# Four packed products in place of eight in the blockwise triangular inverse of a gated DeltaNet and MoBA block

## What is computed

```python
lower = jnp.where(tri_strict, jnp.einsum('bhnid,bhnjd->bhnij', kbc, kc) * decay, 0.0)
eye = jnp.eye(c, dtype=jnp.float32)
t_mat = lax.linalg.triangular_solve(eye + lower, jnp.broadcast_to(eye, lower.shape),
                                    left_side=True, lower=True, unit_diagonal=True)
u = jnp.einsum('bhnij,bhnje->bhnie', t_mat, vbc)
w = jnp.einsum('bhnij,bhnjd->bhnid', t_mat, kbc * jnp.exp(gc)[..., None])
```

## Time and profile before

| | |
|---|---|
| median of 3 runs | 378.04 us |
| the profiled execution | 377.91 us |
| its span (first to last instruction) | 376.1 us |
| TensorE busy | 365.6 us, 97% |
| VectorE busy | 262.9 us, 70% |
| ScalarE busy | 220.1 us, 59% |
| GpSimd busy | 58.0 us, 15% |

### The profile page before, as it was taken

The page is one execution under the profiler, slowest core; times in us unless marked ns, Lnnn a source line. Parts: engine busy times, 40 slices in busy tenths (PEclk is TensorE's granted clock), DMA queues, the critical chain, the costliest instruction groups (busy, mean ns, idle before and its releaser), DMA issues.

```text
span 376.1 us, 7709 instructions
## 1 busy us (share of the span) xinstructions
PE 365.6 (97%) x2821; PEld 349.4 (93%) x2821; DVE 262.9 (70%) x502; ACT 220.1 (59%) x500; POOL 58.0 (15%) x105
## 2 busy tenths in 40 slices
PE   7999999999999999999999999999999999999993
PEld 5889978899999999999999999999999999999882
DVE  2968977299876767867678577786775557677644
ACT  5776894355456565756657577656676644424531
POOL 3435764510120001002020101001010100000000
PEclk9999999999999999999999999999999999999999
DMA  8849746975986465444655445564446656775532
GB/s 265 227 124 298 263 128 163 243 195 143 235 203 180 119 176 155 112 115 115 173 131 142 114 114 126 136 187 114 113 112 165 174 158 176 195 223 197 218 117 112
DMA packets 99342, 62.57 MB, mean 166 GB/s; under 512 B 3652, under 2 KB 94062, under 8 KB 99310
## 3 DMA queue, kind: packets, MB, share of 16 engines
q1 hardware_dynamic: 98014, 58.72, 56.5%
q0 software_dynamic: 1296, 3.43, 3.1%
HBM read 60.55 MB, written 1.59 MB: 165 GB/s over the span
## 4 chain that ended last, share of the span: by engine, by line
PE 89%; ACT 4%; DVE 3%; issue 1%; DMA 1%; POOL 1%; DVEq 0%; POOLq 0%; ACTq 0%
PE banks L1235 64%; PE banks L1452 6%; PE banks L1252 5%; ACT th_E L666 1%; PE banks L1334 1%; PE banks L1367 1%; PE banks L1372 1%; PE banks L1341 1%; PE banks L1352 1%; DVE acc L925 1%; DMA xin<-in_x_dram 1%; PE banks L1377 1%; ACT h_hi L639 1%; PE banks L1382 1%; DVE w_lo L853 1%
## 5 line engine op out<-in xcount | busy, mean ns | idle before, releaser
L1235 PE MATMUL banks<-h_hi,w_hi 128*128 128x256 f32 x576 | 165.6, 288 | 0.6 <-PE banks L1252 0.3
L1235 PE MATMUL banks<-h_lo,w_hi 128*128 128x256 f32 x576 | 165.5, 287 | 0.0
L1235 PE MATMUL banks<-h_hi,w_lo 128*128 128x256 f32 x576 | 165.1, 287 | 0.0
L853 DVE TENSOR_TENSOR w_lo<-raw,w_hi 128x1024 fp32r<-128x1024 f32 x102 | 124.2, 1221 | 35.2 <-ACT w_hi L626 32.3
L626 ACT CAST w_hi<-raw 128x1024 fp32r<-128x1024 f32 x104 | 107.6, 1045 | 9.6 <-DMA raw<-in_w_in_dram 5.0
L1235 PEld LDWEIGHTS banks<-h_hi,w_hi 128*128 128x128 f32 x576 | 110.0, 191 | 2.1 <-issue 1.8
L1235 PEld LDWEIGHTS banks<-h_hi,w_lo 128*128 128x128 f32 x576 | 110.0, 191 | 0.1
L1235 PEld LDWEIGHTS banks<-h_lo,w_hi 128*128 128x128 f32 x576 | 110.0, 191 | 0.2
L925 DVE SCALAR_TENSOR_TENSOR acc<-banks,vec,acc 128x255 f32<-128x255 f32 (+2 forms) x72 | 34.5, 479 | 10.4 <-ACT acc L722 8.1
L1235 PE MATMUL banks<-y_hi,w_hi 128*128 128x256 f32 x128 | 36.2, 283 | 0.0
L1235 PE MATMUL banks<-y_lo,w_hi 128*128 128x256 f32 x128 | 36.2, 283 | 0.0
(11 more groups left out here) (232 smaller groups left out, 547.2 us busy)
## 6 DMA issues: line engine op xcount, KB each, us to landing
raw<-in_w_in_dram SPq DMA_DIRECT2D x80, 512.0 KB, 5.2
raw<-in_w_branch_dram SPq DMA_DIRECT2D x16, 512.0 KB, 4.4
raw<-in_w_out_dram SPq DMA_DIRECT2D x8, 512.0 KB, 4.2
xin<-in_x_dram SPq DMA_DIRECT2D x2, 512.0 KB, 3.7
xin<-bias_rows POOLq DMA_DIRECT2D x1, 1024.0 KB, 7.5
th_E<-g_rows POOLq DMA_DIRECT2D x2, 512.0 KB, 5.8
raw<-in_x_dram SPq DMA_DIRECT2D x2, 512.0 KB, 3.5
out_dram<-xin SPq DMA_DIRECT2D x4, 256.0 KB, 2.1
```

The lines of the kernel that those rows point to most:

```text
L853: v.tensor_tensor(w_lo[:, t % SLOTS, cols], raw[:, t % SLOTS, cols], w_hi[:, t % SLOTS, cols].bitcast(F32), ALU.subtract).then_inc(s_lo, 1)
L1235: last = mm(ps, w, r, start=i == 0, stop=i == 23)
```

## The change

Each of the four product steps of `stage_u` becomes one product of 128 packed columns on either side. The left operand of the steps s = 1 and s = 6 is a packed copy `lac` of the blocks of `la` that count, which GpSimd makes with two copies of 128 x 128 a head (`compact`); the right operand picks its columns by a strided view. In the result the blocks that are wanted lie scattered over lanes and columns, and VectorE copies them, between lanes where needed, to where they belong. The masks and their multiplications go, and with them two of the tiles of `consts`. `U`'s blocks are written, not added to (they are zero until then).

```diff
+        lac = sb("lac", [P, 2, 2, P])
...
+            def compact(g):
+                if g >= 2:
+                    pool.wait_ge(s_x_p, 2 * g - 2)
+                la = la_all[:, g]
+                pool.tensor_copy(lac[:, g % 2, 0, :].rearrange("p (b c x) -> p b c x", b=2, c=NC),
+                                 la.rearrange("p c (b x) -> p b c x", b=2)[:, :, :, BLK:HALF]).then_inc(s_lac, 1)
+                pool.tensor_copy(lac[:, g % 2, 1, :].rearrange("p (c x) -> p c x", c=NC), la[:, :, HALF:]).then_inc(s_lac, 1)
+                pool.wait_ge(s_lac, 2 * g + 2)
+
+            compact(0)
+            compact(1)
             q_norm(0)
             for g in range(HEADS):
                 o_norm(g)
                 if g + 1 < HEADS:
                     q_norm(g + 1)
+                if g + 2 < HEADS:
+                    compact(g + 2)
...
   VectorE, stage_u
                 s == 2
-                    v.tensor_tensor(xl, chunks(bD[:, 0:256]), copies(C_ML, NC), ALU.mult).then_inc(s_x, 1)
+                    by_block = xl[:, 0, :].rearrange("p (b c j) -> p b c j", b=2, c=NC)
+                    for b in range(2):
+                        v.tensor_copy(by_block[HALF * b + BLK:HALF * b + HALF, :, 0, :],
+                                      bD[HALF * b:HALF * b + BLK, 0:HALF].rearrange("p (b j) -> p b j", b=2)).then_inc(s_x, 1)
+                    v.tensor_copy(by_block[:, :, 1, :], bD[:, HALF:P].rearrange("p (b j) -> p b j", b=2)).then_inc(s_x, 1)
                 s == 5
-                    v.tensor_tensor(U, U, chunks(bD[:, 256:512]), ALU.add).then_inc(s_u, 1)
-                    ve.wait_ge(s_u, 2 * g + 1)
+                    for b in range(2):
+                        for c in range(NC):
+                            lane, col = HALF * b + BLK * c, P + HALF * c + BLK * b
+                            v.tensor_copy(U[HALF * b:HALF * b + BLK, c, HALF * b + BLK:HALF * b + HALF],
+                                          bD[lane:lane + BLK, col:col + BLK]).then_inc(s_u, 1)
+                    ve.wait_ge(s_u, 6 * g + 2)
                 s == 7
-                    v.tensor_tensor(xl[:, :, 0:HALF], bD[:, 0:P].rearrange("p (c n) -> p c n", c=NC),
-                                    copies(C_ML + P, NC)[:, :, 0:HALF], ALU.mult).then_inc(s_x, 1)
+                    for c in range(NC):
+                        v.tensor_copy(xl[HALF:, 1, HALF * c:HALF * c + HALF],
+                                      bD[HALF * c:HALF * c + HALF, 2 * P + HALF * c:2 * P + HALF * c + HALF]).then_inc(s_x, 1)
                 s == 10
-                    v.tensor_tensor(high, high, bD[0:HALF, 256:384].rearrange("p (c n) -> p c n", c=NC),
-                                    ALU.add).then_inc(s_u, 1)
+                    for c in range(NC):
+                        v.tensor_copy(U[0:HALF, c, HALF:],
+                                      bD[HALF * c:HALF * c + HALF, 3 * P + HALF * c:3 * P + HALF * c + HALF]).then_inc(s_u, 1)
...
   TensorE, stage_u
-                    for c in range(NC):
-                        last = mm(bD[:, P * c:P * c + P], la[:, c, :], T[:, c, :], start=True, stop=True)
+                    pe.wait_ge(s_lac, 2 * g + 2)
+                    mm(bD[:, 0:P], lac[:, g % 2, 0, :],
+                       T.rearrange("p c (b x) -> p c b x", b=2)[:, :, :, 0:BLK], start=True, stop=True).then_inc(s_x_p, 1)
-                        last = mm(bD[:, 256 + P * c:384 + P * c], xl[:, c, :], U[:, c, :], start=True, stop=True)
+                    mm(bD[:, P:2 * P], xl[:, 0, :], U.rearrange("p c (b x) -> p c b x", b=2)[:, :, :, BLK:HALF],
+                       start=True, stop=True).then_inc(s_d_p, 1)
-                        last = mm(bD[:, HALF * c:HALF * c + HALF], la[:, c, :], T[:, c, 0:HALF], start=True, stop=True)
+                    mm(bD[:, 2 * P:3 * P], lac[:, g % 2, 1, :], T[:, :, 0:HALF], start=True, stop=True).then_inc(s_x_p, 1)
-                        last = mm(bD[0:HALF, 256 + HALF * c:256 + HALF * c + HALF], xl[:, c, 0:HALF], U[:, c, HALF:],
+                    mm(bD[:, 3 * P:4 * P], xl[:, 1, :], U[:, :, HALF:], start=True, stop=True).then_inc(s_d_p, 1)
```

More of the change, by code:

```diff
@@ L85 @@
 R_GATE, R_PRE, R_ON, ROWS = CONV * 24, CONV * 24 + 16, CONV * 24 + 24, CONV * 24 + 25
-LEVELS = [32, 64]
-C_ID, C_ONE, C_TRI, C_ML = (P * i for i in range(4))
-C_ALL = C_ML + P * len(LEVELS)
+C_ID, C_ONE, C_TRI, C_ALL = (P * i for i in range(4))
 BIAS_W = 384
@@ L96, in shape_constants @@
     parts = [row == col, np.ones((P, P)), row <= col]
-    for b in LEVELS:
-        parts.append((row // (2 * b) == col // (2 * b)) & (row // b == col // b + 1))
     consts = np.concatenate([m.astype(np.float32) for m in parts], axis=1)
@@ L215, in build @@
         tri = cst[:, C_TRI:C_TRI + P]
-        def copies(col, count):
-            return cst[:, col:col + P].rearrange("p (a n) -> p a n", a=1).to_broadcast([P, count, P])
         def tap(k, w, h):
@@ L298, in build @@
         s_mdiag = sem("s_mdiag")
+        s_lac = sem("s_lac")
         s_mx = sem("s_mx")
@@ L1077, in stage_u @@
                     ve.wait_ge(s_x_p, 2 * g + 2)
-                    v.tensor_tensor(xl[:, :, 0:HALF], bD[:, 0:P].rearrange("p (c n) -> p c n", c=NC),
-                                    copies(C_ML + P, NC)[:, :, 0:HALF], ALU.mult).then_inc(s_x, 1)
+                    for c in range(NC):
+                        v.tensor_copy(xl[HALF:, 1, HALF * c:HALF * c + HALF],
+                                      bD[HALF * c:HALF * c + HALF, 2 * P + HALF * c:2 * P + HALF * c + HALF]).then_inc(s_x, 1)
                 elif s == 10:
                     ve.wait_ge(s_d_p, 2 * g + 2)
-                    ve.wait_ge(s_u, 2 * g + 1)
-                    high = U[0:HALF, :, HALF:]
-                    v.tensor_tensor(high, high, bD[0:HALF, 256:384].rearrange("p (c n) -> p c n", c=NC),
-                                    ALU.add).then_inc(s_u, 1)
+                    for c in range(NC):
+                        v.tensor_copy(U[0:HALF, c, HALF:],
+                                      bD[HALF * c:HALF * c + HALF, 3 * P + HALF * c:3 * P + HALF * c + HALF]).then_inc(s_u, 1)
             def stage_w(g, s):
@@ L1357, in stage_u @@
             def stage_u(g, s):
-                U, T, la = u2[g % 2], T_all[:, g], la_all[:, g]
+                U, T = u2[g % 2], T_all[:, g]
                 if s == 1:
+                    pe.wait_ge(s_lac, 2 * g + 2)
                     pe.wait_ge(s_turned, g + 1)
                     if g:
-                        pe.wait_ge(s_u, 2 * g)
+                        pe.wait_ge(s_u, 6 * g)
                     else:
                         pe.wait_ge(s_k0, HEADS)
-                    for c in range(NC):
-                        last = mm(bD[:, P * c:P * c + P], la[:, c, :], T[:, c, :], start=True, stop=True)
-                    last.then_inc(s_x_p, 1)
+                    mm(bD[:, 0:P], lac[:, g % 2, 0, :],
+                       T.rearrange("p c (b x) -> p c b x", b=2)[:, :, :, 0:BLK], start=True, stop=True).then_inc(s_x_p, 1)
                 elif s == 4:
-                    pe.wait_ge(s_x, 2 * g + 1)
-                    for c in range(NC):
-                        last = mm(bD[:, 256 + P * c:384 + P * c], xl[:, c, :], U[:, c, :], start=True, stop=True)
-                    last.then_inc(s_d_p, 1)
+                    pe.wait_ge(s_x, 5 * g + 3)
+                    mm(bD[:, P:2 * P], xl[:, 0, :], U.rearrange("p c (b x) -> p c b x", b=2)[:, :, :, BLK:HALF],
+                       start=True, stop=True).then_inc(s_d_p, 1)
                 elif s == 6:
                     pe.wait_ge(s_u12, 2 * g + 2)
-                    for c in range(NC):
-                        last = mm(bD[:, HALF * c:HALF * c + HALF], la[:, c, :], T[:, c, 0:HALF], start=True, stop=True)
-                    last.then_inc(s_x_p, 1)
+                    mm(bD[:, 2 * P:3 * P], lac[:, g % 2, 1, :], T[:, :, 0:HALF], start=True, stop=True).then_inc(s_x_p, 1)
                 elif s == 9:
-                    pe.wait_ge(s_x, 2 * g + 2)
-                    for c in range(NC):
-                        last = mm(bD[0:HALF, 256 + HALF * c:256 + HALF * c + HALF], xl[:, c, 0:HALF], U[:, c, HALF:],
-                                  start=True, stop=True)
-                    last.then_inc(s_d_p, 1)
+                    pe.wait_ge(s_x, 5 * g + 5)
+                    pe.wait_ge(s_u, 6 * g + 4)
+                    mm(bD[:, 3 * P:4 * P], xl[:, 1, :], U[:, :, HALF:], start=True, stop=True).then_inc(s_d_p, 1)
             def stage_w(g, s):
@@ L1388, in stage_w @@
                 if s == 0:
-                    pe.wait_ge(s_u, 2 * g + 2)
+                    pe.wait_ge(s_u, 6 * g + 6)
                     pe.wait_ge(s_vb, 2 * g + 2)
```

## The result

The changed kernel takes 372.38 us (median of 4 runs, 372.23 to 373.05) against 378.01 us before (4 runs beside it): ratio 0.9848, 95% interval 0.9836 to 0.9861. That is 5.6 us faster; 7.2 were forecast. Its profiled execution took 373.05 us with a span of 371.3, the longest of its runs.

A forecast was written before the change was run, and what follows sets the result against it. TensorE's own work was taken as the bound: 8.2 us saved on products, about 1.0 given back at waits, net 7.2 from the profiled 377.9 gives 370.7, predicted as a 370.8 us median; range 369.2 to 373.2 (the forecast's own: 369.2 to 372.8).

The forecast's parts named there:

- What bounds the kernel: Stage of the inverses: TensorE's own work bounds it, busy 365.6 of 376.1 us; removed product cost comes off the end.
- The price of a product: TensorE's four product steps: 0.22 us per product whatever its columns; 1.03 saved a head, 8.2 us over 8 heads.
- columns: Rival, 5%: the saving goes with the product columns, 256 of 768 a head; 375.0 us.
- a slow strided operand: Rival, 3%: each packed product costs as much as a pair, 0.43 in place of 0.22; 377.2 us.
- Where the 0.36 of step 9 comes from: Step 9, TensorE's pair L1382 on 64 lanes: 0.58 becomes 0.22 with one product on all lanes, saving 0.36 a head.
- What TensorE will wait for: TensorE's waits at step 10, step 6 and GpSimd-related places: 0.5 + 0.1 + 0.25 + 0.1 + 0.1, about 1.0 us given back.
- the recurrence in head 5: First product on `stage_w` (L1393 before) waits for step 10's two VectorE copies: 0.5 us back, 0.1 for one other head.
- step 6 in head 7: TensorE's step 6 waits for step 5's four VectorE copies and the transposes: 0.25 us back, 0.1 for one like it.
- the transpose ahead of step 9: L1417 waits for the chain through `o_norm`, as TensorE reaches it 0.45 us sooner: 0.1 us back.
- The price of a copy: VectorE's copies from PSUM: 0.2 us for 64 columns, 0.17 for 32; 2.1 against 1.4 us a head.
- Copies at L1090's price: Rival, 12%: every VectorE copy costs 0.28 us, giving back about 2 us more; 372.8 us.
- GpSimd: GpSimd's `lac` copies: four take 0.8 to 3.6 us, done by 112.5 at the latest, ahead of use; cost 0.

The follow-up runs named there:

- wide_step6: The kernel before the change, with step 6's two products 128 columns wide in place of 64: 378.06 us against 378.25 (0.9998).
- level2_packed: The changed kernel with only the second level (steps 6, 7, 9, 10) packed, the first as before the change: 374.63 us, 0.9910 of before.
- full_lanes: The kernel before the change, with step 9's two products on all 128 output lanes in place of 64: 377.34 us, 0.9978 of before.
- same_lanes: The changed kernel with VectorE's copies reading the lanes they write, or nearly so (values wrong): 371.18 us, 0.9815 of before, 1.2 less than the change.
- gpsimd_more: The changed kernel with four more 128 x 128 GpSimd copies a head into a tile nobody reads: 372.23 us, 0.9845 of before.

## Why the prediction was right, and where it was off

- *The time*: 372.38 lies in the range of 369.2 to 373.2, but nearer to its dear end than to the forecast of 370.8. One of the prediction's own signs of being wrong came true: waits of TensorE of more than 2 us. The other two did not (0.4 for a packed product, over 0.3 for a copy).
- *What bounds the kernel*: right. TensorE's chain was the end before, and all of the gain is in it.
- *The price of a product*: right. 0.22 for each of the four steps, and all rivals about it fell: columns (wide_step6, level2_packed), a slow strided operand (the chain). TensorE's busy time fell by 5.2 us and not by 7 to 8; it holds most of the new waits.
- *Where the 0.36 of step 9 comes from*: right as a number; full_lanes shows that 0.1 of it, 0.9 us over 8 heads, belongs to the 64 lanes. The prediction held this possible ("since it now uses all lanes") and had no test of it.
- *What TensorE will wait for*: the places were right (the recurrence in head 5 and one more, step 6 in head 7 and one more, the transpose ahead of step 9), the size was not. This is the term that failed: about 1.0 us was put down, and it was 2.6 (less 0.1 that was there before). Step 6 made up most of the difference: 0.35 was forecast and 1.2 measured, in four heads and not two. The prediction worked out head 7 and put down one more like it. In the trace of the kernel before, the transposes end 0.47, 0.69, 0.63 and 0.35 us ahead of TensorE in heads 0, 1, 6 and 7. The forecast's prices take 0.3 + 0.23 = 0.53 of that, which leaves heads 1 and 6 something; the measured ones take 0.41 + 0.23 = 0.64, which leaves them next to nothing. So the price of a copy decided how many heads wait. One wait was missed: L1409, 0.24 in head 4, for ScalarE's work on the product that had itself been late.
- *The price of a copy*: the step under it. I took 0.2 and 0.17 us, between the durations of a transpose and of a wide copy; the spacings are 0.24 and 0.21, since copies that turn to other lanes don't overlap. The rival *Copies at L1090's price* (0.28 a copy, 12%) was nearer in its result (372.8) than the forecast (77%), and right in its kind, dearer copies, though not in the price. The rule of the Trainium skill that was quoted for this stood beside the sum without a part in it, and it was the right one: without the change of lanes (same_lanes) some 1.3 us of waits are left, near the 1.0 that was forecast. VectorE is busier by 7.7 us and not by 5.6.
- *GpSimd*: right, cost 0; its copies are mostly 0.23 apart and 10 us early.
- *The start*: 128 KB less to load showed no gain; 0 was taken. The account closes to 0.1 us without it.

## What to carry to other kernels

When an engine is full to the last product, price what is removed by the distance between starts around it, and look at what the neighbours pay too: the half-lane product showed a third of its cost in the instructions behind and ahead of it. Then take each wait that the faster engine comes closer to, head by head, and subtract both its own gain and the slower producer's loss; 2.6 of 8.2 us went there, and six of the eight waits stand where the kernel before had 0.06 to 0.7 us to spare. Replacing one wide operation by several small ones that change lanes costs their full durations one after the other, and it is the last of them that the other engine waits for.

## What the runs showed of the hardware that was not expected

- An fp32 product with 64 x 64 output (64 columns in the left operand, so 64 lanes) costs more than the same with 128: 0.58 against 0.45 for a pair between projection products, and 0.9 us of the whole kernel in full_lanes. Its weight loads are twice as fast, 0.055 us apart, but 0.3 us of pauses stand around them.
- The left-over time of a shorter product is not returned: 64 and 128 columns on the right take the same 0.22 us in this stream (wide_step6, 0.9998), and the weight loads stand 0.11 apart in both.
- Copies from PSUM by VectorE start 0.24 us apart when they turn to other lanes and 0.14 when they don't, at 64 columns (same_lanes).
- GpSimd's copy of 128 x 128 between SBUF tiles lasts 0.29 us; the two of the change that start while VectorE runs a split (L861, 1.22 us, two inputs) last 1.18 and 1.30, the five of gpsimd_more that do so 1.28 to 1.37, and of all others in both runs only one lasts over 0.3 (0.75).
